# A one-core decoder pass on Trainium2: the expert stage joins the block before it, its token choice is rearranged, and the softmax steps inside two dense stages become fewer and wider

## The reference, cut to what matters

```python
# second layer: attention from each token to 256 memory rows, 4 heads of 64
s = einsum('bthd,bmhd->bhtm', q, k) * 64 ** -0.5
m_out = einsum('bhtm,bmhd->bthd', softmax(s), v)
# third layer: 8 heads in 2 key groups, each token sees |i - j| <= 128, with a sink
scores = where(abs(qi - kj) <= 128, q @ k.T / 8, -inf)
m = max(scores.max(), sink); e = exp(scores - m)
probs = e / (e.sum() + exp(sink - m))
# experts: 16 experts, each takes the 64 tokens with the highest affinity for it
aff = softmax(xn @ w_router)                       # 512 x 16
top_aff, top_idx = top_k(aff.T, 64)
xg = xn[top_idx]
y = (silu(xg @ w_gate[e]) * (xg @ w_up[e])) @ w_down[e] * top_aff
h = h.at[top_idx].add(y)
h = h + sigmoid(rmsnorm(h) @ w_ple_gate) * (p @ w_ple)    # the embedding product
```

## Time and profile before

| what | value |
|---|---|
| median of three runs | 2272.54 us (2269.9 to 2273.22) |
| time of the profiled execution | 2273.17 us |
| its span | 2271.4 us |
| PE busy | 2193.3 us, 97% |
| DVE, ACT busy | 654.0 us and 535.3 us |
| mean granted clock of TensorE | 0.988 |
| DMA | 317.40 MB, 409 GB/s in the slices of the expert stage |

### The profile page before, as it was taken

The page is one execution under the profiler, slowest core; times in us unless marked ns, Lnnn a source line. Parts: engine busy times, 40 slices in busy tenths (PEclk is TensorE's granted clock), DMA queues, the critical chain, the costliest instruction groups (busy, mean ns, idle before and its releaser), DMA issues. The chain is left out here.

```text
span 2271.4 us, 19765 instructions
## 1 busy us (share of the span) xinstructions
PE 2193.3 (97%) x8040; PEld 1049.9 (46%) x8040; DVE 654.0 (29%) x1107; ACT 535.3 (24%) x1037; POOL 0.2 (0%) x4
## 2 busy tenths in 40 slices
PE   9999999999999999999999999999989989999897
PEld 5455565544444454444444455554454333333333
DVE  3455534322212223311342344421130010100134
ACT  3645443310001322211123324320121000000022
POOL 0000000000000000000000000000000000000000
PEclk9999999999999999999999999999989999999998
DMA  9211211122222210222221211212348999999951
GB/s 232 58 38 38 71 41 61 47 97 74 74 74 83 75 46 21 63 77 66 75 75 38 74 38 38 75 48 74 148 167 304 409 409 409 410 409 409 409 199 37
DMA packets 164602, 317.40 MB, mean 140 GB/s; under 512 B 44800, under 2 KB 74624, under 8 KB 164512
## 3 DMA queue, kind: packets, MB, share of 16 engines
q1 hardware_dynamic: 162480, 314.41, 38.4%
q10 hardware_dynamic: 2032, 1.73, 0.3%
HBM read 314.01 MB, written 2.10 MB: 139 GB/s over the span
## 5 line engine op out<-in xcount | busy, mean ns | idle before, releaser
L417 PE MATMUL bank<-hT,ring 128*128 128x512 f32 (+1 forms) x1632 | 736.0, 602 | 10.7 <-PEq L442 5.8
L417 PEld LDWEIGHTS bank<-hT,ring 128*128 128x128 f32 (+1 forms) x1632 | 304.7, 192 | 368.4 <-issue 360.0
L417 PE MATMUL bank<-ring,hT 128*128 128x512 f32 (+2 forms) x576 | 219.0, 539 | 0.0
L2287 PE MATMUL bank<-wide,xg 128*64 128x512 f32 x600 | 179.2, 596 | 9.7 <-DMA ring<-in_w_exp_gate 2.5
L417 PEld LDWEIGHTS bank<-ring,hT 128*128 128x128 f32 x576 | 103.6, 191 | 106.9 <-issue 103.4
L2287 PE MATMUL bank<-ring,xg 128*64 128x512 f32 x392 | 132.9, 596 | 4.6 <-DMA ring<-in_w_exp_gate 3.4
L417 PE MATMUL bank<-rz,ring 128*128 128x512 f32 x256 | 111.3, 593 | 0.0
L2287 PEld LDWEIGHTS bank<-wide,xg 128*64 128x64 f32 x600 | 54.7, 137 | 97.3 <-issue 96.3
L2322 PE MATMUL bank<-wide,hidT 128*64 128x512 f32 x304 | 89.4, 596 | 6.4 <-ACT hidT L2378 3.5
L417 PEld LDWEIGHTS bank<-rz,ring 128*128 128x128 f32 x256 | 48.8, 191 | 61.1 <-issue 60.8
L2413 DVE TENSOR_TENSOR xT<-bank,xT 128x512 f32<-128x512 f32 x32 | 22.1, 692 | 176.0 <-PE bank L2213 175.9
(11 more groups left out here) (433 smaller groups left out, 2215.0 us busy)
## 6 DMA issues: line engine op xcount, KB each, us to landing
wide<-in_w_exp_gate SPq DMA_DIRECT2D x76, 512.0 KB, 12.4
wide<-in_w_exp_down SPq DMA_DIRECT2D x76, 512.0 KB, 14.0
wide<-in_w_exp_up SPq DMA_DIRECT2D x74, 512.0 KB, 13.2
ring<-in_l_w_in SPq DMA_DIRECT2D x18, 2048.0 KB, 7.8
ring<-in_w_exp_gate SPq DMA_DIRECT2D x52, 512.0 KB, 12.4
ring<-in_w_exp_down SPq DMA_DIRECT2D x52, 512.0 KB, 13.2
ring<-in_w_exp_up SPq DMA_DIRECT2D x46, 512.0 KB, 13.5
ring<-in_w_in SPq DMA_DIRECT2D x10, 2048.0 KB, 7.9
```

The source lines that it names most:

```text
L417: mm = pe.matmul(self.out(n), *mats[i], start=i == 0, stop=i == len(mats) - 1)
L2287: mm = pe.matmul(bank[2 * which + n][e * 64:(e + 1) * 64, :], xg[p // 2 % 2][:, k, s:s + CAP], block_ap(j)[k % 2][:, n * 512:(n + 1) * 512 ...
```

## The change

1. **Memory attention:** a unit is now one token tile with both head pairs: 4 units instead of 8, each twice as wide. Two probability buffers instead of three. The retention stages begin four steps earlier.
2. **Banded attention:** for the first and the last token tile a unit holds two head pairs: 12 units instead of 16. The 16 dense jobs are cut in quarters of two matmuls (64) and spread over the 12 steps.
3. **One block** from `Linear` to the end: branches, experts, last products and stores follow each other by semaphores alone. The last products wait for `ye_out` and `put_out`.
4. **Token choice:** all of logits 5, 6, 7 behind the last job; DVE copies the logits; ACT loads its tables ahead with two tiny activations and makes the exponentials before the row copies; the affinities are transposed after row tile 2; the first max round reads PSUM; the chosen mask is transposed by itself and multiplied after the transposes of the scan; the one-hot columns come in two halves, and the first gather waits for the first.
5. **Embedding:** five tiles there, three between gate and up of the first pair. The first pair's `gather_first` of the second pair goes behind up; a gather of pairs 2 and 3 goes from up to down.
6. **Places:** blocks are given to places in a written-out order (`LIMIT`, `EMB`): 13 blocks before the first expert matmul, the embedding's place is given to block 21, one more place up to block 71 (so block e waits for block e-11 there). Blocks 5 to 12 no longer wait for the end of a block of the program.

```diff
-        units = [(t, i) for t in range(TT) for i in range(2)]
+        units = list(range(TT))
...
+                        for i in range(2):
+                            for e in range(2):
+                                r = slice(e * 64, (e + 1) * 64)
+                                mm = pe.matmul(psum[:, 2 + e, i * MEM:(i + 1) * MEM], eq[i][r, t * P:(t + 1) * P],
+                                               memk[1][r, i, :], start=True, stop=True)
...
-                        if s >= 3:
-                            act.wait_ge(m_turn, s - 2)
+                        if s >= 2:
+                            act.wait_ge(m_turn, s - 1)
...
-        units = [(t, i) for t in range(TT) for i in range(4)]
+        units = [(t, i, n) for t in range(TT) for n in ((2,) if t in (0, TT - 1) else (1,)) for i in range(0, 4, n)]
+        quarters = [(n, k, k + 2) for n in range(len(jobs)) for k in range(0, KD, 2)]
+        plan = [quarters[len(quarters) * s // NU:len(quarters) * (s + 1) // NU] for s in range(NU)]
...
+        EMB, EMB_TO = 13, 7
+        LIMIT = {9: 16, 10: 16, 11: 3 * NB, 12: NB}
+        order = list(range(E0))
+        waiting = [(n, None) for n in range(EMB)]
+        for e in range(NB * len(EXP)):
+            n, by = waiting.pop(0)
+            while e >= LIMIT.get(n, e + 1):
+                n, by = waiting.pop(0)
+            j = E0 + e
+            order.append(j)
+            wide_at[j] = places[n]
+            taken_from[j] = by if by in (None, "embedding") else E0 + by
+            waiting.append((n, e))
+            if e == EMB_TO:
+                waiting.append((EMB, "embedding"))
...
+        for i in range(4):
+            place_free[5 + i] = (tiles_done, last_tile[WO2[i // 2]])
+        for i in range(3):
+            place_free[9 + i] = (tiles_done, last_tile[WO2[1]])
+        place_free[12] = (sums_t, 1)
+        place_free["embedding"] = (ple_t, KD)
...
-                logits(pe, (6, 7)).then_inc(logit_t, 1)
...
+                for m in range(5):
+                    pe.wait_ge(*((rows_out, 5 + m) if m < 4 else (pw_out, 1)))
+                    embedding_part(m, bank[1 + m % 4])
+                pe.wait_ge(mask_ready, 1)
...
-                pe.wait_ge(pw_out, 8)
+                pe.wait_ge(pw_out, 3)
...
+                        if p == 0 and which == 1:
+                            pe.wait_ge(pw_out, 5)
+                            for m in range(5, KD):
+                                embedding_part(m, bank[m - 1])
...
+                    if p == 0:
+                        pe.wait_ge(pw_out, KD)
+                        for c in range(2):
+                            gather_first(1, c, bank[4 + c])
...
+                dve.wait_ge(logit_t, 1)
+                dve.tensor_copy(lgT, bank[7][0:NE, :]).then_inc(lgT_out, 1)
...
+                left = bank[5][0:NE, :]
                 for _ in range(CAP // 8):
-                    step(dve.max(top[:, :], work))
-                    step(dve.match_replace(work, top[:, :], work, -1.0))
...
+                    step(dve.max(top[:, :], left))
+                    step(dve.match_replace(work, top[:, :], left, -1.0))
+                    left = work
...
+        for m in range(8):
+            jobs[m]["needs"] = [(put_out, NP), (ye_out, 2 * NP - 1 if m < 4 else 2 * NP)]
...
-        run_products(jobs, end_sync=store)
...
+        run_stages(Linear, branches, Experts, Products(jobs), Store)
```

More of the change, by code:

```diff
@@ L332, in issue_blocks @@
         def issue_blocks(sp, upto):
-            while issued[0] < min(upto, len(stream)):
-                j = issued[0]
+            while issued[0] < min(upto, len(order)):
+                j = order[issued[0]]
                 issued[0] += 1
+                dst, src = block_ap(j), stream[j][0]
                 if j < WPL:
@@ L436, in take, with run_stages, _, __init__ @@
                     job[kind + "_then"](eng, self.done_at[n])
+        def run_stages(*stages):
+            with nc.Block() as block:
+                @block.sync
+                def _(sp):
+                    for x in stages:
+                        x.sync(sp)
+                @block.tensor
+                def _(pe):
+                    for x in stages:
+                        x.tensor(pe)
+                @block.scalar
+                def _(act):
+                    for x in stages:
+                        x.scalar(act)
+                @block.vector
+                def _(dve):
+                    for x in stages:
+                        x.vector(dve)
+        class Products:
+            def __init__(self, jobs, upto=None):
+                self.dense, self.upto = Jobs(jobs, range(6)), upto
+            def sync(self, sp):
+                self.dense.issue(sp, self.upto)
+            def tensor(self, pe):
+                for n in range(len(self.dense.jobs)):
+                    self.dense.product(pe, n)
+            def scalar(self, act):
+                for n in self.dense.order:
+                    self.dense.take(act, "act", n)
+            def vector(self, dve):
+                for n in self.dense.order:
+                    self.dense.take(dve, "dve", n)
         def run_products(jobs, begin=None, upto=None, end_sync=None, abreast=0):
@@ L1764, in _ @@
                     if s < NU:
-                        dense.take(act, "act", s)
+                        for n, k, end in plan[s]:
+                            if end == KD:
+                                dense.take(act, "act", n)
                     if 1 <= s <= NU:
@@ L2196, in unit_at, with sync, tensor @@
             return placed[p] + sum(len(x) for x in combined(p)[:place])
-        with nc.Block() as block:
-            @block.sync
-            def _(sp):
+        class Experts:
+            @staticmethod
+            def sync(sp):
                 issue_blocks(sp, len(stream))
-            @block.tensor
-            def _(pe):
+            @staticmethod
+            def tensor(pe):
                 def combine(p, place):
```

357 lines of the change are left out of this document (192 added, 165 removed).

## The result

The changed kernel takes 2259.24 us (median of 4 runs, 2257.13 to 2260.93), the kernel before 2271.97 us beside it (4 runs, 2269.9 to 2273.22). The ratio is 0.9944 with a 95% interval of 0.9927 to 0.9962: 12.7 us faster. The profiled execution of after took 2260.93 us, span 2259.1; that of before had a span of 2271.4, so the two traces are 12.3 us apart. The prediction was 2260, with 12.3 as its sum.

What follows compares the result with a forecast made beforehand. PE was taken to bound the kernel up to the first expert matmul, then the stream of weights. Memory -2.7, banded -0.7, stream (with the choice) -8.0 and last products -0.9 sum to -12.3 us: 2260 us, range 2254 to 2266.

Steps and rivals of the forecast that it cites:

- Bound and rule for the sum: Whole kernel: time of first expert matmul, plus the stream's idle time behind it, plus 2.56 us per block still to load.
- Memory steps: Memory attention, 8 steps to 4: each step dropped saves 0.68 us of changes between kinds of matmul; -2.7 us.
- Banded steps: Banded attention, 16 steps to 12: fewer changes, but a longer last chain; net -0.7 us, ends -2.7 and +2.
- Token choice: From sums of squares to experts: earlier logits and affinities bring the first expert matmul from 1700.22 to 1689.6, -10.6 us.
- The rival in which the clock is still at half when the embedding starts: Token choice: two embedding tiles at half speed make the ranks wait 2.3 us for PE; 2262 us, 3 in 100.
- Stream: Expert weights: one block more to load (+2.6 us), idle time the same, so the stream ends at -8.0 us.
- The eleventh place and the three moved embedding tiles: Expert stage: both costed at nothing, the tiles' 5.2 us on PE being covered by 16.3 us of waits for weights.
- PE takes the expert stage: Rival, expert stage: PE becomes the bound and the three embedding tiles count in full; 2263 us, 13 in 100.
- Last products: End of the experts: the end of the block goes, PE waits only for the first of two copies; -0.9 us.
- At 2256: Rival, stream and sums: today's idle time reckoned 2 us short and the clock's fall both go; 2256 us, 11 in 100.
- The wider steps bring nothing: Rival, both attention stages: with two buffers for three PE waits as much as it saves; 2264 us, 11 in 100.
- The slower one: Rival, expert stage: the clock falls to half in waits for weights; 2289 us with 90 us at half speed, 3 in 100.

Runs made afterwards that it cites:

- filled choice: Changed kernel plus four products of 512 columns, read by nobody, in PE's waits of the token choice; 2254.36 us.
- tiles_back: Changed kernel with all eight embedding tiles in the token choice, none in the first pair of experts; 2254.83 us.
- mem_only: Kernel before with only the memory attention's part of the change (8 units to 4); 2266.82 us.
- band_fill: Changed kernel plus five products of 512 columns, read by nobody, in PE's wait before the last banded transposes; 2257.7 us.
- band_only: Kernel before with only the banded attention's part of the change (16 steps to 12); 2269.97 us.

## Why the prediction was right, and where it was not

**Bound and rule for the sum: right, but for one sentence.** The time of the first expert matmul, then the stream behind it: the first expert matmul comes 39.87 us behind the sums in before and 27.25 with the filled choice, and from there the stream takes 448.28 and 448.54 us. PE still waits for weights at 2137.01 us. Inside the choice the chain on DVE sets the time more than PE does: PE waits 1.69, 0.83 and 1.19 us for it. The sentence that a microsecond of PE work saved behind the first expert matmul is worth nothing while there are waits for weights is wrong: in the run tiles_back 5.2 us of such work were taken out of the first pair, and the last wait came 5.1 us earlier.

**Memory steps: right.** -2.5 for -2.7, shown alone. PE meets a wait of 0.21 us in one step, where the prediction had it covered (its 3.9 us have the peak on DVE in them, which it does not name).

**Banded steps: this term was mis-sized.** "Net -2.7 + 3.1 - 1.1 = -0.7 us" was measured as +2.0 in this pair of traces, its upper end. The wait grew from 2.83 to 4.79, as it said ("nearly 5"). What it left out is the clock behind the wait. In after, 5.5 us of tail and part of the next block's products ran at 0.50; with PE kept at work the stretch is 1.9 us shorter than before. How much of the +2.0 belongs to the edit stays open: the two traces with the old code have 344.61 and 347.84 us (mean 346.2), the eight with the banded stage of after 345.03 to 346.62 (mean 346.2 too), so they show neither a gain nor a loss. What decides how long the clock stays low, I did not find; the wait's length alone does not. The steps themselves may have been reckoned well, by an estimate: at 1.00 the old tail would take 0.46 us less for its transposes (1.12 against the 0.66 of mem_only) and some 0.84 less for its values (1.98 against half of the 2.28 of band_fill), which makes 343.3, and the new one has 342.75 with the clock kept up: -0.6, for -0.7.

**Token choice: right, with its steps.** Behind the sums of squares:

| | predicted, us | after, us |
|---|---|---|
| transposes of the affinities | 4.7 | 3.94 |
| first max | 5.3 | 4.58 |
| transposes of the ranks | 19.0 | 18.25 |
| first gather | 20.5 | 19.90 |
| first expert matmul | 29.5 | 29.79 |

The chain was 0.7 us faster than reckoned and the gather 0.96 slower than the 9.01 taken from the earlier trace rows, for the clock. Of the -10.1, some is scatter of before: the same old code has 39.87, 38.16 and 39.62 us in three traces. The rival in which the clock is still at half when the embedding starts did not come. From 1662 to 1664, on transposes, the granted clock was 1.00, and the five tiles took 8.75 us, 1.75 each. That does not test the rule of the Trainium skill on transposes (TensorE: Matmul & The Clock Gate, Part 4: PE-mode transpose), for here the clock had not fallen ahead of them. In the run band_only it had, and it went from 0.50 (1664 to 1668) to 0.80 (1668 to 1670) and 1.00 while PE ran transposes alone (1664.27 to 1670.23), as in before: the traces do not agree with the rule. The half clock came later, in the waits behind the embedding.

**Stream: the term was mis-sized.** "So the stream ends at -10.6 + 2.6 = -8.0 us" counted one block more to load and equal idle time. The idle time was indeed 16.4 where 15.9 was said, but the stretch is 0.8 shorter in this pair of traces. Part of the difference is scatter: with the stage unchanged it took 448.28, 446.03 and 447.22 us (mean 447.2), and with the stage of after 447.47, 447.49, 448.02, 448.19, 448.54 and 447.59 (mean 447.9). On the means the stream costs 0.7 us, which is +2.6 for the block and -1.9 for the idle time of the two traces (18.3 to 16.4); by the mean idle times (17.8 to 16.6) the rule would give +1.4. The prediction reckoned 16 us for the 18.3 of before, and those 2 us are its error. The pair of traces adds 1.5 in the kernel's favour, which I take for scatter.

**"The eleventh place and the three moved embedding tiles (5.2 us on PE) are thus costed at nothing": wrong.** The waits for weights do not cover the tiles. They lie ahead of block 16's end, and so inside the chain that releases block 27: PE's time in the first pair is stream time. The reckoning of the gaps had the tiles in it (block 16 done at 47), so the sum did not suffer, but the sentence is wrong by +5.1 and -2.7. The rival "PE takes the expert stage" counted the tiles in full, but PE did not take the stage. Four pieces were measured, one trace each: tiles +5.1, place -2.7, order of the gathers -2.6, 13 blocks for 14 +0.4 (this one with the eight tiles in the choice). They sum to +0.2, between the +0.7 of the means and the -0.8 of the pair of traces.

**Last products: right.** -0.8 for -0.9: PE waits 0.98 us for DVE's first copy.

**The other rivals.** At 2256: the idle time of today was indeed 2 us short, and the clock no longer fell at the sums (they took 1.05 us for 1.68), but it fell at the gather instead. "The wider steps bring nothing": the two terms of steps gave -0.5 together, but not for its reason; PE did not wait as much as it saved in the steps. The slower one did not come: behind waits of up to 1.5 us for weights the granted clock stayed at 1.00. It did fall twice in the stage, behind the waits of 2.01 us for DVE, but for some 7 us at half speed in all, not the 57 from which it decides. The cases below 2268 that hold 93 in 100 are five, not four.

## What to carry to other kernels

Where a queue of loads is released by the work of an engine, count what that engine does ahead of each release: such work is on the path even when the engine waits elsewhere. A wait of PE costs what stands in its row, and at times the clock of what follows; so put work that must be done anyway into the waits, and price the rest by the row at 1.2 GHz. When a sum comes out right, read its terms by marks in both traces: here two errors of 3 us cancelled, and no time of the whole kernel shows that.

## What the runs showed of the hardware

The cost of the same wait differs between executions. Behind 2.82 or 2.83 us of idle PE the same code ran its next block's first stretch in 11.52 us once and in 15.31 once; the code of after took 13.22 and, in the run with the filled choice, 11.52. Behind 4.79 us of idle PE after lost 3.8 us in all, and with five products in the wait none. The clearest case is the gather behind the wait of 2.01 us, twice in each of the 14 traces: 14 of the 28 took 3.69 us and 14 took 5.38, and nothing in between. Waits for weights of up to 1.5 us in after, and of up to 2.18 in the other runs, were followed by no such fall. And code that is the same in all kernels reached the memory stage between 722.5 and 726.4 us, so single spans that differ by less than 4 us tell nothing here without marks inside the trace.
